# Context's down product from split operands, and modulation sums of two units per instruction

## Time and profile before

| | |
|---|---|
| time, median of 3 runs | 2030.86 us (2030.85 to 2031.01) |
| the profiled execution's own time | 2030.74 us |
| its span, first to last instruction | 2028.9 us |
| TensorE busy | 1991.8 us (98%) |
| VectorE busy | 1247.4 us (61%) |
| ScalarE busy | 758.8 us (37%) |
| GpSimd busy | 509.8 us (25%) |
| mean granted TensorE clock | 0.993 |

### The profile page before, as it was taken

How to read it: one execution, slowest core, us unless ns; L and a number is a source line. 1 busy time by engine, 2 the same in 40 slices (tenths; PEclk the granted TensorE clock), 3 DMA queues, 4 the chain that set the end, 5 groups by cost and what they waited for, 6 DMA issues and landing times.

```text
span 2028.9 us, 26082 instructions
## 1 busy us (share of the span) xinstructions
PE 1991.8 (98%) x10112; PEld 1686.5 (83%) x10112; DVE 1247.4 (61%) x1887; ACT 758.8 (37%) x1098; POOL 509.8 (25%) x371
## 2 busy tenths in 40 slices
PE   7999999999999999999999999999999999999997
PEld 5999988888888888888989898877788888888886
DVE  5987766556788678776252334459556555555555
ACT  4333533333333345455111222346333333334342
POOL 2000043333212102124232322664332421210001
PEclk9999999999999999999999999999999999999998
DMA  8974426656556787733001011221665654566664
GB/s 330 353 274 137 156 91 221 213 195 225 203 190 215 262 298 239 253 119 100 27 21 42 32 58 47 65 82 57 213 202 208 218 163 148 167 212 196 192 194 156
DMA packets 108763, 343.53 MB, mean 169 GB/s; under 512 B 11488, under 2 KB 20960, under 8 KB 90464
## 3 DMA queue, kind: packets, MB, share of 16 engines
q1 hardware_dynamic: 108640, 341.85, 49.3%
HBM read 267.36 MB, written 74.45 MB: 168 GB/s over the span
## 4 chain that ended last, share of the span: by engine, by line
PE 90%; DVE 4%; ACT 2%; issue 1%; DMA 1%; POOL 0%; DVEq 0%; POOLq 0%; SPq 0%; ACTq 0%
PE PS L2150 12%; PE PS L2152 12%; PE PS L2151 12%; PE PS L1992 8%; PE PS L1994 8%; PE PS L1993 8%; PE PS L2192 7%; PE PS L2194 7%; PE PS L2193 7%; PE PS L2108 4%; DVE WVL L1583 1%; PE PS L2368 1%; PE PS L2049 1%; DMA WR<-w_units 1%; PE PS L2029 0%
## 5 line engine op out<-in xcount | busy, mean ns | idle before, releaser
L2150 PE MATMUL PS<-HH,WVH 128*128 128x512 f32 x672 | 262.5, 391 | 0.1
L2152 PE MATMUL PS<-HH,WVL 128*128 128x512 f32 x672 | 261.6, 389 | 0.0
L2151 PE MATMUL PS<-HL,WVH 128*128 128x512 f32 x672 | 261.5, 389 | 0.0
L1992 PE MATMUL PS<-HH,WH 128*128 128x512 f32 x416 | 164.9, 396 | 4.0 <-DVE WL L1774 4.0
L748 POOL TENSOR_TENSOR WL<-WR,WH 128x512 fp32r<-128x512 f32 x80 | 108.7, 1386 | 213.9 <-ACT WH L927 159.5
L1994 PE MATMUL PS<-HH,WL 128*128 128x512 f32 x416 | 162.0, 389 | 0.0
L1993 PE MATMUL PS<-HL,WH 128*128 128x512 f32 x416 | 162.0, 389 | 0.0
L1583 DVE TENSOR_TENSOR WVL<-WR,WVH 128x512 fp32r<-128x512 f32 x160 | 115.3, 721 | 69.7 <-ACT WVH L1010 68.2
L2150 PEld LDWEIGHTS PS<-HH,WVH 128*128 128x128 f32 x672 | 126.3, 188 | 26.5 <-ACT U L1042 0.5
L2152 PEld LDWEIGHTS PS<-HH,WVL 128*128 128x128 f32 x672 | 126.1, 188 | 26.3
L2151 PEld LDWEIGHTS PS<-HL,WVH 128*128 128x128 f32 x672 | 126.2, 188 | 26.2
(11 more groups left out here) (282 smaller groups left out, 4806.7 us busy)
## 6 DMA issues: line engine op xcount, KB each, us to landing
WR<-w_units SPq DMA_DIRECT2D x89, 1024.0 KB, 5.8
gated<-HB SPq DMA_DIRECT2D x44, 512.0 KB, 6.5
down_weight_sums<-WB SPq DMA_DIRECT2D x22, 1024.0 KB, 3.8
gated_sums<-TBF SPq DMA_DIRECT2D x22, 768.0 KB, 4.1
AW<-ada_units SPq DMA_DIRECT2D x12, 1024.0 KB, 13.0
HLF<-down_weight_sums SPq DMA_DIRECT2D x46, 256.0 KB, 3.4
W2RB<-w_units SPq DMA_DIRECT2D x22, 512.0 KB, 3.6
WB<-w_units SPq DMA_DIRECT2D x22, 512.0 KB, 3.6
```

The lines of the kernel that those rows point to most:

```text
L1992: pe.matmul(dst, wh, xh, start=first, stop=False)
L2150: pe.matmul(bank[:, :], wh, xh, start=first, stop=False, skip_group_check=True)
L2151: pe.matmul(bank[:, :], wh, xl, start=False, stop=False, skip_group_check=True)
L2152: ins = pe.matmul(bank[:, :], wl, xh, start=False, stop=k == 3, skip_group_check=True)
```

```diff
-ADA_SUMS = (15, 14, 14, 14) + (11,) * 7 + (9, 12, 12, 12, 13)
+ADA_PAIR = 14
+ADA_SUMS = (5, 6, 6, 6) + (5,) * 11 + (6,)
+ADA_FIRST_ADDS = {0: 0, 1: 1, 4: 2, 6: 3, 9: 4, 12: 5}
...
-    return 16 * len(ADA_DVE) + sum(ADA_SUMS[:max(0, p + 1)])
+    return sum(ADA_SUMS[:max(0, p + 1)])
 
 
 def ada_units_done(p):
 
-    return 8 - len(ADA_DVE) + ada_sums_done(p) // 16
+    return 8 + 2 * (ada_sums_done(p) // ADA_PAIR)
+
+def sums_place(j):
+    return ((j + 1) // 2 % 2, (j + 1) % 2) if j else (0, 0)
...
-        AW = [at(f"AW{j}", [P, KT, UC], F32, (HIGHS, LOWS)[j // 4] + 8192 * (j % 4)) for j in range(8)]
-        AS = at("AS", [P, 3, 2, UC], F32, R + 24576)
-        ROWS = at("ROWS", [4, 2, UC], F32, R + 30720)
+        AWP = [at(f"AWP{j}", [P, 2, KT, UC], F32, (HIGHS, LOWS)[j // 2] + 16384 * (j % 2)) for j in range(4)]
+        AW = [AWP[j // 2][:, j % 2] for j in range(8)]
+        AS = at("AS", [P, 2, 2, 2, UC], F32, R + 24576)
+        ROWS = at("ROWS", [4, 2, UC], F32, R + 42496)
         AWL = {n: at(f"AWL{n}", [P, KT, UC], F32R, LOWS + 8192 * (n % 4)) for n in ADA_SPLIT}
-        CSS = at("CSS", [P, KT, 4], F32R, R + 40960)
-        SEL = at("SEL", [4, 2], F32, R + 41216)
+        CSS = at("CSS", [P, KT, 4], F32R, R + 41472)
+        SEL = at("SEL", [4, 2], F32, R + 41728)
         XCB = at("XCB", [P, KT, CTX], F32, R + 32768)
-        HCHB = at("HCHB", [P, KT, CTX], F32R, R + 49152 + 448)
-        HCLB = at("HCLB", [P, KT, CTX], F32R, R + 57344 + 448)
-        W2RB = at("W2RB", [P, 2, D], F32, R + 66560)
-        PR = at("PR", [P, 2, CTX], F32, R + 74752)
-        SG = at("SG", [P, CTX], F32, R + 76800)
+        HCHB = at("HCHB", [P, KT, CTX], F32R, R + 49152 + 64)
+        HCLB = at("HCLB", [P, KT, CTX], F32R, R + 57344 + 64)
+        W2R, W2L, W2H = [], [], []
+        for j, o in enumerate((32768, 65664)):
+            W2R.append(at(f"W2R{j}", [P, D], F32, R + o))
+            W2L.append(at(f"W2L{j}", [P, D], F32R, R + o))
+            W2H.append(at(f"W2H{j}", [P, D], F32R, R + o + 4096))
+        PR = at("PR", [P, 2, CTX], F32, R + 73920)
+        PRL = at("PRL", [P, 2, CTX], F32R, R + 73920)
+        PRH = at("PRH", [P, 2, CTX], F32R, R + 75968)
...
+                if p == 0:
+                    sp.wait_ge(s_xm, 8 * (J[0, 0] + 1))
+                sp.dma_start(W2R[p % 2][:, :], w2_units[p]).then_inc(s_w2raw[p % 2], 16)
...
-            ctx_down_unit(0)
             ctx_down_unit(1)
             ada(9)
+            ctx_down_unit(0)
...
+                    sp.wait_ge(s_yb, NF - 1)
+                    tokens_in(0)
...
+            def first_adds(q):
+                a, (r, u) = 8 + 2 * q, sums_place(2 * q + 1)
+                for e in range(2):
+                    act.wait_ge(s_first[a % 8 + e], load_count(a))
+                act.wait_ge(s_col, 2 * q + 6 if q > 1 else 4)
+                for v in range(2):
+                    act.activation(AS[:, r, v, :, :], AWP[a % 8 // 2][:, :, 0, :], ACT.Copy,
+                                   scale=CS[:, 0, v:v + 1]).then_inc(s_as0, 1)
+            def ctx_product_high(p):
+                act.wait_ge(s_prod, p + 1)
+                act.activation(PRH[:, p % 2, :], PR[:, p % 2, :], ACT.Copy).then_inc(s_rh, 1)
             for p in range(NF):
                 if p:
                     act.wait_ge(s_gu, p)
                 high(p % 2, 16 * ((p + 1) // 2 + 1))
+                if p:
+                    ctx_product_high(p - 1)
+                else:
+                    first_adds(0)
+                act.wait_ge(s_w2raw[p % 2], 16 * (p // 2 + 1))
+                act.activation(W2H[p % 2][:, :], W2R[p % 2][:, :], ACT.Copy).then_inc(s_rh, 1)
                 act.wait_ge(s_gu, p + 1)
-                if p:
-                    act.wait_ge(s_prod, p)
-                act.activation(SG[:, :], PS[p % 2][:, 0:CTX], ACT.Silu).then_inc(s_silu, 1)
+                if p >= 2:
+                    act.wait_ge(s_yb, p - 1)
+                act.activation(PR[:, p % 2, :], PS[p % 2][:, 0:CTX], ACT.Silu).then_inc(s_silu, 1)
+                if p and p in ADA_FIRST_ADDS:
+                    first_adds(ADA_FIRST_ADDS[p])
...
+            def pair_sum(n):
+
+                q, i = divmod(n, ADA_PAIR)
+                k, v, (r, u) = 1 + i // 2, i % 2, sums_place(2 * q + 1)
+                if k == 1:
+                    dve.wait_ge(s_as0, 2 * q + v + 1)
+                else:
+                    dve.wait_ge(s_asum, 15 + (ADA_PAIR - 1) * q + i - 1)
+                dst = AS[:, r, v, :, :]
+                ins = dve.scalar_tensor_tensor(dst, AWP[(8 + 2 * q) % 8 // 2][:, :, k, :], CS[:, k, v:v + 1], dst,
+                                               ALU.mult, ALU.add)
+                if i == ADA_PAIR - 1:
+                    ins.then_inc(s_adv, 2)
+                else:
+                    ins.then_inc(s_asum, 1)
...
+            def ctx_product_low(p):
+                dve.wait_ge(s_rh, 2 * p + 2)
+                dve.tensor_tensor(PRL[:, p % 2, :], PR[:, p % 2, :], PRH[:, p % 2, :].bitcast(F32),
+                                  ALU.subtract).then_inc(s_rl, 1)
             for p in range(NF):
                 block_low(p + 1)
+                if p:
+                    ctx_product_low(p - 1)
                 if p and ada_units_done(p - 2) > ada_units_done(p - 3):
                     dve.wait_ge(s_col, ada_units_done(p - 2))
                     for a in range(ada_units_done(p - 3), ada_units_done(p - 2)):
                         ctx_mods(a)
                 for n in range(ada_sums_done(p - 1), ada_sums_done(p)):
-                    ada_sum(n)
+                    pair_sum(n)
...
+                dve.wait_ge(s_rh, 2 * p + 1)
+                dve.tensor_tensor(W2L[p % 2][:, :], W2R[p % 2][:, :], W2H[p % 2][:, :].bitcast(F32),
+                                  ALU.subtract).then_inc(s_rl, 1)
                 dve.wait_ge(s_silu, p + 1)
-                if p >= 2:
-                    dve.wait_ge(s_yb, p - 1)
-                dve.tensor_tensor(PR[:, p % 2, :], SG[:, :], PS[p % 2][:, CTX:2 * CTX], ALU.mult).then_inc(s_prod, 1)
+                dve.tensor_tensor(PR[:, p % 2, :], PR[:, p % 2, :], PS[p % 2][:, CTX:2 * CTX], ALU.mult).then_inc(s_prod, 1)
+            ctx_product_low(NF - 1)
...
+                r, u = sums_place(j)
                 for c in range(4):
                     t, v = c // 2, c % 2
                     ins = pe.matmul(PS[6][:, 16 + 4 * (n % 4) + c:17 + 4 * (n % 4) + c],
-                                    AS[:, j % 3, v, t * P:(t + 1) * P], ONES[:, 0:1], start=True, stop=True)
+                                    AS[:, r, v, u, t * P:(t + 1) * P], ONES[:, 0:1], start=True, stop=True)
...
             def ctx_down(p):
 
-                pe.wait_ge(s_prod, p + 1)
-                pe.wait_ge(s_w2raw[p % 2], 16 * (p // 2 + 1))
+                pe.wait_ge(s_rl, 2 * p + 2)
                 for d in range(KT):
                     dst = PS[2 + d // 2][:, d % 2 * CTX:(d % 2 + 1) * CTX]
-                    ins = pe.matmul(dst, W2RB[:, p % 2, d * P:(d + 1) * P], PR[:, p % 2, :],
-                                    start=p == 0 and d % 2 == 0, stop=p == NF - 1, skip_group_check=True)
+                    wh, wl = (t[p % 2][:, d * P:(d + 1) * P] for t in (W2H, W2L))
+                    pe.matmul(dst, wh, PRH[:, p % 2, :], start=p == 0 and d % 2 == 0, stop=False, skip_group_check=True)
+                    pe.matmul(dst, wh, PRL[:, p % 2, :], start=False, stop=False, skip_group_check=True)
+                    ins = pe.matmul(dst, wl, PRH[:, p % 2, :], start=False, stop=p == NF - 1, skip_group_check=True)
                 ins.then_inc(s_yb, 1)
```

More of the change, by code:

```diff
@@ L68 @@
 NSLOT = 6
+CTX_OPERANDS = 2 * NF
 MAJOR = 4
@@ L1430, in ada_sum @@
                 else:
-                    dve.wait_ge(s_asum, 15 * j + 2 * k + v - 1)
+                    dve.wait_ge(s_asum, 2 * k + v - 1)
                     ins = dve.scalar_tensor_tensor(dst, w, c, dst, ALU.mult, ALU.add)
-                ins.then_inc(s_adv if n % 16 == 15 else s_asum, 1)
+                ins.then_inc(s_adv if n == 15 else s_asum, 1)
+            def pair_sum(n):
[12 more added lines that the diff above has]
+                    ins.then_inc(s_asum, 1)
             def latent_sums(a, half):
-                sums, links = sums_count(a - 1), 15 * sums_count(ADA_CTX - 1) + 6 * (a - ADA_CTX)
+                sums, links = sums_count(a - 1), 15 + (ADA_PAIR - 1) * (ADA_CTX - 8) // 2 + 6 * (a - ADA_CTX)
                 unit, acc, _ = latent_places(a)
@@ L1472, in _ @@
             for n in range(8):
-                ada_sum(n)
+                first_sum(n)
             ada_rows(2)
             for n in range(8, 16):
-                ada_sum(n)
+                first_sum(n)
             ada_mods(1)
```

34 lines of the change are left out of this document (15 added, 19 removed).

## The result

The changed kernel takes **2044.57 us** (median of four runs, 2044.10 to 2045.49) beside 2030.93 us (four runs, 2030.85 to 2032.51) for the kernel before on the same chip: 1.0069 times as long, 95% interval 1.0057 to 1.0082. That is 13.6 us slower. I had said 2037 us with a range of 2027 to 2046. The direction and the place were right, the loss of 6.3 us was a little under half of what came.

What follows compares the result with a forecast made beforehand. It took TensorE to set the pace before, and VectorE's list after turn 1's stall: 72.5 + 165.8 + 18 = 256.3, plus 10.9 of TensorE, end at 267.2 against 260.94, +6.3 us on 2030.74, so 2037 us, range 2027 to 2046.

Steps and rivals of the forecast that it cites:

- The stall of turn 1: Turn 1 of the context stage: ScalarE waits for unit 11's load, so TensorE waits 10 us for product 1's low part.
- The clock behind it: After the wait in turn 1, TensorE does about 5 us of work at half speed, 2.4 us lost.
- VectorE's list: From 72.5 us to product 20's low part: 165.8 us of work plus 18 us idle, ready at 256.3.
- Turn 6: Turn 6 of the context stage: 2.8 us of VectorE idle time, where ScalarE waits for unit 15.
- turns 15 to 18: Late context stage: 8.2 us of VectorE idle time, as ScalarE starts the high part only 5.75 us after the SiLU.
- in time for the SiLU: Down unit loads: each lands 3.6 us after down product p - 2, the SiLU comes 5.46 us after that; costs nothing.
- What TensorE saves: Down products of the context stage: 2.73 us instead of 3.45, 0.72 us a turn, 15.8 us in 22 turns.
- the promised gain: Rival, chance 0.08: unit 11 lands early or the wait is elsewhere, TensorE stays the bound, 2015 us.
- The stall alone: Rival, chance 0.19: TensorE waits at turn 1 (10 + 2.4 us) but VectorE keeps up after, 2028 us.
- Worse on VectorE: Rival, chance 0.13: VectorE's sums or low parts run longer than their kin, 10 to 15%, 2048 us or more.

Runs made afterwards that it cites:

- e1: The changed kernel with the loads of modulation units 10 and 11 moved ahead of the first turn's token loads: 2036.65 us.
- e2: The changed kernel with ScalarE making the first products of units 10 and 11 in turn 2 instead of turn 1, loads unmoved: 2037.14 us.
- e8b: The changed kernel with 90 products that nothing reads, run by TensorE ahead of the second down product: 2044.78 us.
- e3: The changed kernel with its pair sums kept but the plain float32 down product of before, without high and low parts: 2042.58 us.
- e10: The changed kernel with pair sums, the plain float32 down product of before and the early load of units 10 and 11: 2034.28 us.
- e7: e1 with 10 of the 14 pair sums of each pair of modulation units left out, so an incomplete computation: 2031.21 us.
- e9: e1 with the SiLU ahead of the down unit's high part on ScalarE, and the product ahead of its low part on VectorE: 2038.04 us.
- e12: e7 with the SiLU ahead of the down unit's high part on ScalarE: 2037.34 us.
- e4: The changed kernel with the split down product kept but the old modulation sums, one unit per instruction, all on VectorE: 2042.04 us.
- e11: e1 with the split down product only in turns 0 to 13 and the plain float32 one in turns 14 to 21: 2031.53 us.
- e13: e11 with the SiLU ahead of the down unit's high part on ScalarE: 2033.31 us.
- e5: The changed kernel with the low part of the down unit computed by GpSimd instead of VectorE: 2065.26 us.

## Why the prediction was right in its direction and short in its size

**The stall of turn 1: right.** 10.50 us against 10, by the chain that I had named. e1 and e2 take it away in two ways and win 7.9 and 7.4 us.

**The clock behind it: right in kind and size; what it costs at the end is not shown.** From 73.32 us on TensorE does 5.4 us of work at the lower clock, some 2.7 us lost against the forecast 2.4. e8b took this away and the time stayed, but in its profile other waits and falls of the clock took its place. The Trainium skill, "TensorE: Matmul & The Clock Gate", section "HAM oscillation — how this bites in real kernels", has each long wait followed by a cold start; here it holds for the 10.50 us wait, not for each of the shorter ones (below).

**VectorE's list: its work right, its idle time mis-sized.** The step was: from 72.5 us the list holds 165.8 us of work, and 18 us of idle time come on top. One row of stretches, from the low part of product 1 to the end of that of product 20, gives what it was:

```profile
72.85:261.92 189.07, 179.82 (x1484) 177.43 (x1484) 164.50 (x231) 111.30 (x149) 2.02 (x2) 0.98 0.60 215
```

VectorE works for 164.50 us, 1.3 less than forecast. It is idle for 189.07 - 164.50 = 24.6 us, not 18. So the low part of product 20 comes at 261.9 instead of 256.3, 5.6 us late, and that is nearly the whole gap: the stage ends 12.3 us after that of before, the forecast was 6.3. Most of the missing idle time is in two places that I had seen and taken too small; some 2 us more are small gaps, the largest 1.04 us in turn 20. Turn 6, forecast 2.8 us, has 4.06, and turns 15 to 18, forecast 8.2, have 5.99 + 2.91 + 2.29 = 11.2. The rows of VectorE, and under them those of ScalarE that stand behind the first:

```profile
118.07 1.49 DVE L1359 TENSOR_TENSOR ACC<-ACC,SQX 128x512 f32<-128x512 f32 x2 [4.06 <-ACT SQX L957]
...
210.89 2.29 DVE L1515 TENSOR_TENSOR WL<-WR,WH 128x2048 fp32r<-128x2048 f32 x1 [5.99 <-ACT WH L943]
```

```profile
113.70 1.06 ACT L1016 ACTIVATE W2H<-W2R 128x1024 fp32r<-128x1024 f32 x1 [5.23 <-DMA W2R<-w_units]
...
116.18 1.34 ACT L1000 ACTIVATE AS<-AWP,CS 128x512 f32<-128x512 f32 x2 [1.15 <-issue]
```

In turn 6 ScalarE first waits for the down unit, 5.23 us, a load that I had put at nothing ("in time for the SiLU"), and then for unit 15. In turn 15 there is a wait that I overlooked altogether: the token work of ScalarE stands until VectorE's last pair sum is done (1.86 us), and the high part of the next unit stands behind it. VectorE was busy for 87% of that row's stretch, where I had said over 90% of the stage. The remaining 1.3 us of the 13.6 lie after the stage, below.

**What TensorE saves: mis-sized, 0.63 us a turn and not 0.72, and a part of it given back.** I had read 3.45 us for the old down product and 0.114 us from start to start for the split ones from a turn of 8.91 us. The first holds, the second does not hold for every turn. The timeline of TensorE in the kernel before, in the turn that I had read and in a later one with the same work:

```profile
102.52 3.62 PE L2108 MATMUL PS<-PR,W2RB 128*128 128x256 f32 x16
105.79 0.47 PE L1992 MATMUL PS<-HCHB,WH 128*128 128x256 f32 x1
106.10 0.28 PE L1993 MATMUL PS<-HCLB,WH 128*128 128x256 f32 x1
106.22 0.28 PE L1994 MATMUL PS<-HCHB,WL 128*128 128x256 f32 x1
...
111.44 0.38 PE L2108 MATMUL PS<-PR,W2RB 128*128 128x256 f32 x1
```

```profile
212.34 3.61 PE L2108 MATMUL PS<-PR,W2RB 128*128 128x256 f32 x16
215.61 0.47 PE L1992 MATMUL PS<-HCHB,WH 128*128 128x256 f32 x1
215.91 0.28 PE L1993 MATMUL PS<-HCLB,WH 128*128 128x256 f32 x1
...
221.45 0.81 PE L2108 MATMUL PS<-PR,W2RB 128*128 128x256 f32 x3
```

and the changed kernel:

```profile
181.96 0.28 PE L2172 MATMUL PS<-PRH,W2H 128*128 128x256 f32 x1
...
184.78 0.28 PE L2055 MATMUL PS<-HCHB,WH 128*128 128x256 f32 x1
184.90 0.28 PE L2056 MATMUL PS<-HCLB,WH 128*128 128x256 f32 x1
```

The old down product (16 records for 8 in the code) takes 3.27 us to the next start, and the second product behind it comes 0.31 us after the first instead of 0.12: 3.46 in all, as the chain of waits has it. Behind that, the products of gate and up start 0.114 us apart in the first turn (106.10 to 111.44, 47 of them) and 0.118 in the second (215.91 to 221.45), so that the same work takes 8.92 us and 9.11. The new down product is 24 times 0.118, 2.83 us, with no late product behind it. Where nothing waits, as from 182.16 to 190.64 in the changed kernel (SiLU of turns 13 and 14, gate and up at 0.118), a turn is 8.48 us long: **0.63 less than 9.11**, 13.9 us in 22 turns and not 15.8. A part of this goes back, since the closer starts become rarer: gate and up have them in 10 of 21 whole turns of the stage before, in 5 with the change, in none of e3 and e10. What makes them closer in one turn and not in the next no run shows; that the addresses moved, which I had priced at nothing, can be the reason as well as another. In the sum the saving hardly counted, as VectorE set the end, but the rivals hung on it, and so did what I expected of e7, e9 and e12.

The change of a stage's length (SiLU of turn 0 to the adding of the last context products, before: 212.4 us) is made of TensorE's waits, half of its work at the low clock, and what its own work became shorter or longer. The last is what is left of the measured change without the other two:

| kernel | waits | low clock | measured | own work |
|---|---|---|---|---|
| the change | 19.7 | 4.4 | +12.8 | -11.3 |
| e1, unit 11 early | 12.8 | 1.7 | +5.0 | -9.5 |
| e2, first products late | 12.7 | 3.4 | +6.1 | -10.0 |
| e3, plain down product | 6.4 | 4.5 | +12.8 | +1.9 |
| e10, the same, early | 0 | 1.7 | +3.6 | +1.9 |
| e4, old sums | 17.7 | 4.8 | +11.9 | -10.6 |
| e7, few sums | 9.9 | 1.7 | +0.5 | -11.1 |
| e12, and SiLU first | 12.4 | 4.8 | +6.6 | -10.6 |
| e9, SiLU first | 13.0 | 4.7 | +7.0 | -10.7 |
| e11, plain tail | 6.5 | 0 | +0.9 | -5.6 |
| e13, and SiLU first | 7.1 | 0 | +1.5 | -5.6 |
| e5, low part on GpSimd | 30.9 | 13.4 | +32.7 | -11.6 |

(Low clock: over stretches of 2 us, busy time times one less the granted clock. Each row is the one execution of the profile; those of e1 and e11 took 2.6 us less than their medians.) The last column is much the same wherever all 22 down products are split, -9.5 to -11.6, about half of it with 14 split turns, and +1.9 where none is: there the ten turns that have lost the closer starts, 0.19 us each, account for it. e8b with its 10.4 us of idle products fits too (17.8 - 11.8 - 10.4 - 6.0 = -10.4). Worked out from the turns, 22 times 0.63 less the lost closer starts, the split kernels should have -12.4 to -13.3; the 1 to 3 us between the two stay open. So the change gives TensorE 11.3 us, and against that stand 10.5 us in which one late load holds ScalarE's queue, 9.2 us in seven shorter waits for `PRL`, and 4.4 us of the clock that falls behind such waits. With the stall and its clock alone the stage would be 10.5 + 2.7 - 11.3 = 1.9 us longer; the seven shorter waits and the second fall of the clock make the other 10.9 of the 12.8.

**The bound of the rest.** My picture was that VectorE's work sets the pace after the stall. e4 and e11 speak for it: more work on it lengthens TensorE's waits, and less of it in turns 14 to 21 ends them. e7 speaks against it as the whole: 10 of 14 sums gone, and TensorE's waits only fall from 12.8 to 9.9 us, at the same places (turns 2, 3, 7, 10, 16, 18 and 21). Most of these are places where a fixed list has something late ahead of the product: table loads, unit 15, a trip to GpSimd, token work. The split makes them matter, since it puts four instructions of two engines (`PRH`, `W2L`, `WL`, `PRL`) between the product of gate and up and the down product, where there were none. Which of them gives how much stays open.

**Of the rivals,** the promised gain fell with the first trace. The stall alone (2028) is refuted by e1: without the stall the kernel is still 6 us behind the one before. Worse on VectorE (2048 or more) by longer instructions did not come, as 743 and 1217 ns show.

## What to carry to other kernels

When work moves to an engine with time to spare, look at its queue and not at its share: one load that lands late held ScalarE for 13 us and with it everything behind, and a table entry one turn later won 7 us back. Price a group of pipelined instructions by the distance between starts in both kernels over a whole turn, and look at more than one turn first: here two turns of one kernel with the same work took 8.92 and 9.11 us, and a comparison of unlike ones (8.92 with 8.48) hides a third of the saving. And when a saving on the bounding engine needs several small steps on two others between producer and consumer, count every late thing ahead of those steps as a wait of the bounding engine.
